# A whole-model kernel on one core: the ends and the beginnings of two attention blocks rearranged

## The reference

```python
for i in range(DEPTH):
    h  = half_ffn(h, ...);  hc = half_ffn(hc, ...)
    u  = modulated_norm(h, g[2], m, 3);  uc = modulated_norm(hc, g[2], mc, 3)
    if kind == 0: y, yc = diff_attention_mixer(u, uc, ...)     # p[:, 0] - lam * p[:, 1]
    elif kind == 1: y, yc = gqa_axial_mixer(u, uc, ...)        # q and k are rms-normed
    h = gated_residual(h, y, g[3], m, 3, 1.0)
    h = half_ffn(h, m, 6, ...)
    if ctx_out:                                                # layer 0 only
        hc = gated_residual(hc, yc, ...);  hc = half_ffn(hc, mc, 6, ...)

def attend(qb, kb, vb):                                        # DA, per head and query block
    sc = einsum('blhid,bkhid->bihlk', qb, kb) * scale
    p = softmax(sc);  p = p[:, 0] - lam_full * p[:, 1]
    o = einsum('bhlk,bkhd->blhd', p, vb)
    return rmsnorm(o, subln) * (1.0 - lambda_init)             # a norm per head
```

## Time and profile before

| | |
|---|---|
| median of three runs | 2476.23 us (2474.5 to 2476.89) |
| the profiled execution's own time | 2472.06 us |
| its span, first to last instruction | 2470.3 us |
| mean granted TensorE clock | 0.984 |
| busy: PE, DVE, ACT, POOL | 2349.1, 1479.4, 913.9, 1363.2 us |
| DMA, mean | 142 GB/s |
| DA, from the first rotary matmul to the last head's sum | 453.2 to 672.9 us |
| GA, from the first sum of squares to the last product with v | 1498.7 to 1597.3 us |

### The profile page before, as it was taken

How to read it: one execution, slowest core, us unless ns; L and a number is a source line. 1 busy time by engine, 2 the same in 40 slices (tenths; PEclk the granted TensorE clock), 3 DMA queues, 4 the chain that set the end, 5 groups by cost and what they waited for, 6 DMA issues and landing times.

```text
span 2470.3 us, 35964 instructions
## 1 busy us (share of the span) xinstructions
PE 2349.1 (95%) x14514; PEld 2073.8 (84%) x14514; DVE 1479.4 (60%) x2344; ACT 913.9 (37%) x1461; POOL 1363.2 (55%) x688
## 2 busy tenths in 40 slices
PE   6999999899899999999999997889989999999998
PEld 5887789677688777898778886789989999999998
DVE  6999896656569998968973045563235212563421
ACT  3222224444442222243222244444444444544443
POOL 4455465122144554554554451268868886466986
PEclk8999999999999999999999998999999999999999
DMA  6555452111125554525533321135536564344554
GB/s 270 196 187 185 145 194 83 60 60 52 37 84 196 193 182 152 185 98 186 180 111 90 101 83 61 68 132 185 178 113 205 179 193 146 101 147 144 190 181 135
DMA packets 97220, 350.09 MB, mean 142 GB/s; under 512 B 10912, under 2 KB 10912, under 8 KB 96800
## 3 DMA queue, kind: packets, MB, share of 16 engines
q1 hardware_dynamic: 97056, 347.81, 41.7%
HBM read 346.71 MB, written 1.05 MB: 141 GB/s over the span
## 4 chain that ended last, share of the span: by engine, by line
PE 50%; DVE 13%; issue 4%; ACT 2%; DMA 1%; POOL 1%; DVEq 0%; ACTq 0%
PE psum L1345 16%; PE psum L1349 15%; PE psum L1346 15%; DVE psum L962 8%; PE psum L1639 1%; DVE sq L1149 1%; POOL w_lo L650 1%; PE psum L1612 1%; DMA ada_lo<-in_ada_w 1%; ACT w_hi L670 0%; DVE gu_hi L1152 0%; DMA w_raw<-in_ffn_in 0%; PE psum L1620 0%; PE psum L1380 0%; DVE h L1058 0%
## 5 line engine op out<-in xcount | busy, mean ns | idle before, releaser
L650 POOL TENSOR_TENSOR w_lo<-w_raw,w_hi 128x1024 fp32r<-128x1024 f32 (+3 forms) x684 | 1363.0, 2011 | 1090.0 <-ACT w_hi L670 1089.2
L1345 PE MATMUL psum<-u_hi,w_hi 128*128 128x256 f32 (+1 forms) x2912 | 978.5, 336 | 20.1 <-DVE sq L1149 6.1
L1349 PE MATMUL psum<-u_lo,w_hi 128*128 128x256 f32 (+1 forms) x2912 | 950.9, 327 | 2.9 <-DVE u_lo L1044 2.9
L1346 PE MATMUL psum<-u_hi,w_lo 128*128 128x256 f32 (+1 forms) x2912 | 949.9, 326 | 0.0
L670 ACT ACTIVATE w_hi<-w_raw 128x1024 fp32r<-128x1024 f32 (+1 forms) x522 | 534.1, 1034 | 422.4 <-PE psum L1349 347.7
L1345 PEld LDWEIGHTS psum<-u_hi,w_hi 128*128 128x128 f32 x2912 | 558.5, 192 | 102.4 <-DVE sq L1149 26.6
L1349 PEld LDWEIGHTS psum<-u_lo,w_hi 128*128 128x128 f32 x2912 | 557.6, 191 | 49.9 <-DVE u_lo L1044 3.9
L1346 PEld LDWEIGHTS psum<-u_hi,w_lo 128*128 128x128 f32 x2912 | 558.7, 192 | 43.7 <-issue 2.9
L1345 PE MATMUL psum<-gu_hi,w_hi 128*128 128x256 f32 (+1 forms) x1188 | 379.3, 319 | 0.0
L1346 PE MATMUL psum<-gu_hi,w_lo 128*128 128x256 f32 (+1 forms) x1188 | 378.2, 318 | 0.0
L1349 PE MATMUL psum<-gu_lo,w_hi 128*128 128x256 f32 (+1 forms) x1188 | 378.1, 318 | 0.0
(11 more groups left out here) (144 smaller groups left out, 1965.9 us busy)
## 6 DMA issues: line engine op xcount, KB each, us to landing
w_raw<-in_ffn_in SPq DMA_DIRECT2D x264, 512.0 KB, 4.1
w_raw<-in_ffn_out SPq DMA_DIRECT2D x96, 448.0 KB, 3.4
ada_hi<-in_ada_w SPq DMA_DIRECT2D x48, 512.0 KB, 3.6
ada_lo<-in_ada_w SPq DMA_DIRECT2D x48, 512.0 KB, 3.5
w_raw<-in_ffn_out SPq DMA_DIRECT2D x48, 512.0 KB, 3.5
ada_out<-in_ada_w SPq DMA_DIRECT2D x32, 512.0 KB, 4.5
w_raw<-in_b_qkv SPq DMA_DIRECT2D x30, 512.0 KB, 3.5
w_raw<-in_da_in SPq DMA_DIRECT2D x24, 512.0 KB, 3.5
```

What stands on the lines that cost most here:

```text
L650: last = pool.tensor_tensor(w_lo[:, slot, w], w_raw[:, slot, w], w_hi[:, slot, w].bitcast(F32), ALU.subtract)
L1345: mm(out, w_hi[:, slot, w], x_hi, start=start and n == 0, stop=False)
L1346: mm(out, w_lo[:, slot, w], x_hi, start=False, stop=False)
L1349: last = mm(out, w_hi[:, slot, w], x_lo, start=False, stop=stop and n == len(ks) - 1)
```

## The change

Five edits, all around the two attention blocks of the first network; `b2` keeps its order.

1. **First phase.** DA gets a fifth tile, k of head 1, as an extra: its latent pass stands ahead of `h_sum`, its context pass behind those of the first four. GA runs k0, v0, k1, v1 (all of the keys and values) as its four and the latent q0 as its extra. The input tiles of GA lie in that order in memory. v1 is staged in an unused part of `q_st`.
2. **DA's last head.** Its units go latent, latent, context, context, and its end (`O`, `oss`) is done once for the latent half and once for the context half, the latter through bank 6.
3. **DA's output** begins with the latent pieces of tiles 2 and 3, ahead of the last k of tiles 0 and 1. The latent pieces of tiles 4 to 7 use banks 4 and 5 in turn, where they used 0, 1, 4, 5.
4. **Fillers.** DA's are spread over the last unit and behind, with none kept; GA begins a third output tile with the heads and keeps three.
5. **Heads.** ACT makes the heads of output tiles 4 and 5 of DA beside the last head's transposes, not in the output.

```diff
@@ -101,11 +101,14 @@
 def out_pieces(kind, tok):
 
     if tok == LAT:
-        return [(j, LAT, {"ffn": 4 + j % 2, "b2": j % 2, "ga": (0, 1, 4, 5)[j % 4]}[kind]) for j in range(CH)]
-    first, banks = (6, (4, 5, 0, 1)) if kind == "ffn" else (2, (4, 5, 0, 1))
-    tail = [(j, half) for half in halves(FULL) for j in range(first, CH)]
-    return [(j, FULL, 4 + j % 2 if kind == "ffn" else j) for j in range(first)] \
-        + [(j, half, banks[i % 4]) for i, (j, half) in enumerate(tail)]
+        banks = {"ffn": (4, 5), "b2": (0, 1), "ga": (0, 1, 2, 4, 5, 0, 1, 4)}[kind]
+        return [(j, LAT, banks[j % len(banks)]) for j in range(CH)]
+    if kind == "ffn":
+        tail = [(j, half) for half in halves(FULL) for j in range(6, CH)]
+        return [(j, FULL, 4 + j % 2) for j in range(6)] + [(j, half, (4, 5, 0, 1)[i]) for i, (j, half) in enumerate(tail)]
+    ctx = slice(0, CTX)
+    return [(2, LAT, 4), (3, LAT, 5), (0, FULL, 0), (1, FULL, 1)] \
+        + [(j, LAT, 4 + j % 2) for j in range(4, CH)] + [(j, ctx, (0, 1, 4, 5)[(j - 2) % 4]) for j in range(2, CH)]
...
-FILL_UNITS = 3
-FILL_KEPT = {"da": 4, "ga": 2, "b2": 0}
+FILL_UNITS = {"da": 1, "ga": 3, "b2": 3}
+FILL_KEPT = {"da": 0, "ga": 3, "b2": 0}
+EARLY = {"da": 2, "ga": 3, "b2": 2}
...
+            tiles = (2, 0, 3, 1) if h < DA_HEADS - 1 else (2, 3, 0, 1)
             sets.append({"s": h, "items": items, "q": items[:1], "k": items[1:2], "v": items[2:],
-                         "units": [{"qt": qt, "keys": keys, "ocol": qt * 128} for qt, keys in
-                                   ((2, TOK), (0, CTX), (3, TOK), (1, CTX))]})
+                         "units": [{"qt": qt, "keys": TOK if qt >= 2 else CTX, "ocol": qt * 128} for qt in tiles]})
     elif kind == "ga":
-        kv = None
+        kv = [[item("k", g, 0, FULL, norm=True, rope=True, par=g), item("v", g, 0, FULL, par=g)] for g in range(GA_KV)]
         for h in range(GA_HEADS):
             g = h // (GA_HEADS // GA_KV)
-            items = []
-            if h % (GA_HEADS // GA_KV) == 0:
-                kv = [item("k", h, 0, FULL, norm=True, rope=True, par=g % 2), item("v", h, 0, FULL, par=g % 2)]
-                items += kv
+            items = [it for pair in kv for it in pair] if h == 0 else []
             items.append(item("q", h, 0, LAT, norm=True, rope=True, par=0, place=h % 3))
-            sets.append({"s": h, "items": items, "q": items[-1:], "k": kv[:1], "v": kv[1:],
+            sets.append({"s": h, "items": items, "q": items[-1:], "k": kv[g][:1], "v": kv[g][1:],
                          "units": [{"qt": qt, "keys": TOK, "ocol": qt * 128} for qt in (2, 3)]})
...
+        if kind == "da" and st["s"] == DA_HEADS - 1:
+            st["outs"] = [{"s": st["s"], "tok": LAT, "after": U - 3}, {"s": st["s"], "tok": slice(0, CTX), "after": U - 1}]
+        else:
+            st["outs"] = [{"s": st["s"], "tok": FULL if kind == "da" else LAT, "after": U - 1}]
+    for n, x in enumerate(x for st in sets for x in st["outs"]):
+        x["n"] = n
+    for n, it in enumerate(it for st in sets for it in st["items"] if it["norm"]):
+        it["sq"] = n
...
+    items = [it for st in sets for it in st["items"]]
+    first, extra = items[:4], items[4:4 if kind == "b2" else 5]
+    begun = set((it["idx"], k) for it in first + extra for k in range(0, CH, 2))
+    add("first", (first, extra))
...
+    lead += parts(ahead)[:{"da": 2, "ga": 4, "b2": 0}[kind]]
     for part in lead:
-        begun.add(part[0]["idx"])
+        begun.add((part[0]["idx"], part[1]))
         add_part(part)
         prepare_due()
...
+        filler += [(d, k, min(k + 2, last), last) for d in range(2, EARLY[kind]) for k in range(0, last, 2)]
     kept = FILL_KEPT[kind]
...
+        if it["what"] == "v" and it["g"] == 0 and it["s"] == 1 and it["idx"] == 3:
+            return q_st[:, 1, 0:n]
...
+        if kind == "da" and s == DA_HEADS - 1 and tok != LAT:
+            return SUMS
...
-                    for it in x:
+                    for it in x[0] + x[1]:
                         evacuate(it)
...
+                    if kind == "da" and u["set"]["s"] == DA_HEADS - 1:
+                        heads_to(min(b["t_out"] + 4 + u["U"] - u["set"]["first_unit"], b["t_out"] + RING - 1))
...
-                    return len(tiles) - n if n == full[-1] else 1
+                    return len(tiles) - n + sum(tok == LAT for _, _, tok in extra) if n == full[-1] else 1
...
-            for t, bank, _ in extra:
-                run(1, t, bank, range(CH)).then_inc(tile_used, 1)
+            for t, bank, tok in extra:
+                if tok != LAT:
+                    run(1, t, bank, range(CH)).then_inc(tile_used, 1)
...
+                if b["kind"] == "da":
+                    ctx_ready = lambda k: pe.wait_ge(MS["da"]["olo_ready"], k + 2)
...
-                early = b["kind"] in ("da", "ga") and i < 2
+                early = b["kind"] in ("da", "ga") and j < EARLY[b["kind"]]
...
-    X["ga_in"] = ga[[n for g in range(GA_KV) for n in (GA_HEADS + g, GA_HEADS + GA_KV + g, *range(per * g, per * g + per))]]
+    X["ga_in"] = ga[[n for g in range(GA_KV) for n in (GA_HEADS + g, GA_HEADS + GA_KV + g)] + list(range(GA_HEADS))]
```

97 lines of the change are left out of this document (50 added, 47 removed).

## The result

The changed kernel takes 2481.71 us (median of 7 executions, 2480.38 to 2485.11), the one before 2475.02 in the same series (2472.99 to 2479.2): ratio 1.0026, interval 1.0016 to 1.0035, so 6.4 us slower (4.0 to 8.7). 2478.5 was forecast, 2.2 us slower than before, with "within 0.2%" (5 us) as the likeliest case. Gains and losses are worked out from these ratios throughout (0.0001 is 0.25 us); the plain difference of the two medians is 6.7. The profiled execution took 2481.71 (span 2479.9). That of before took 2472.06, and all 31 executions of before timed in the next series took longer than that (2472.11 to 2479.73, median 2476.43). The two traces are 9.65 us apart, where the ratio gives 6.4: some 3 us between the traces are luck of the execution.

What follows compares the result with a forecast made beforehand. PE, 95% busy, bounds the blocks' middles; chains through DVE and ACT bound starts and ends. -0.6 + 0.5 + 1.3 + 0.7 + 0.3 = +2.2 us on median 2476.23, about 2478.5; 8-in-10 range 2468.5 to 2488.

Steps and rivals of the forecast that it cites:

- likeliest case: Whole kernel: time within 0.2% (5 us) of before, the sum of the terms with its errors; chance 0.47.
- DA's start: Start of DA: latent pass of the fifth tile fits the idle time; 0.6 us gained, bounds 2.8 gained and 1.5 lost.
- DA's last head: Units 28 to 31 of DA, with no filler between their scores: 0.5 us lost, bounds 3 gained and 2 lost.
- DA's output: Output of DA: 1.3 us of new wait at latent piece 6, bounds 0.4 and 2.5.
- GA's start: Start of GA: unit 2 delayed 13.6 us against 12.9 saved in the middle; 0.7 lost, bounds 5.3 gained, 3 lost.
- k0's Ln: Sign in GA's start: ACT comes to k0's Ln some 7 us later than before.
- GA's end: End of GA: 0.7 us gained by fillers and third output tile, 1.0 lost; net 0.3 lost, bounds 0.8 and -2.
- Rival 1: DA and GA: filled gaps count in full, 11 us gained, 2465; middle version 2471; chance 0.22.
- Rival 2: GA's start: ACT's queue decides; GA loses 5 to 7 us, DA 2 to 3, 2484; chance 0.31.
- Rival 3: GA's first phase: k1 and v1 could put off DVE's work on the context half; no size, called nearly excluded.
- the 2 us at unit 29's scores: Sign in DA's last head: about 2 us of PE idle time between scores of units 28, 29 and 30.
- the 1 to 2 ahead of piece 6: Sign in DA's output: 1 to 2 us of PE idle time before latent piece 6.

Runs made afterwards that it cites:

- e1: Changed kernel with the DA edits alone, GA as before the change; ratio to before 1.0007, 1.7 us slower.
- e10: e4 with the sums of squares of k0, q0 and k1 also put ahead of the transposes of v0 and v1; ratio to before 1.0007.
- e3: Changed kernel with v7's transposes right behind unit 28's scores instead of unit 30's; ratio to before 1.0016, changed kernel 1.0026.
- e8: Changed kernel without ACT's heads of DA's output tiles 4 and 5 beside the last head's transposes, made in the output instead; ratio to before 1.0027.
- e9: Changed kernel with added unused matmuls where PE stands idle in DA's last head; ratio to before 1.0023.
- e4: Changed kernel with ACT's three heads of GA's first phase moved behind the Ln and Exp of k0, q0 and k1; ratio to before 1.0009.
- e7: Changed kernel without GA's third early output tile, two fillers kept; ratio to before 1.0023.
- e12: e10 with v7's transposes right behind unit 28's scores and the heads of DA's output tiles 6 and 7 one piece later; ratio to before 0.9983.
- e2: Changed kernel with the GA edits alone, DA as before the change; ratio to before 1.0016, 4.0 us slower.
- e11: e10 with DA's last head and output as before the change, DA's fifth tile kept; ratio to before 0.9987, 3.2 us faster.

## Why the prediction was right, and where it was not

The direction was right and the time lies in the range, 3.2 us above the likeliest one. The size was not: 6.4 us slower (4.0 to 8.7) where 2.2 were forecast, so the likeliest case, within 5 us, is met only by the lower end of the interval. In the traces DA is 6.8 us longer and GA 5.5; together that is nearly twice the 6.4 of the ratio, so part of what follows is what these two executions happened to get. The terms, by the profiled executions:

- **DA's start**, forecast 0.6 gained. Shown: nothing that can be told from zero (0.3 by the means above; from `h_sum` to unit 28's scores, unit 1 included, 210.2 us as a mean of the twelve, 208.4 to 211.0, against 210.3 and 210.7). That context passes run no sooner was right. Part of the scatter is the clock behind the sum: 0.68 granted in the changed kernel (438.5 to 443), 1.00 in e1 and e10.
- **DA's last head**, forecast 0.5 lost, bounds 3 gained and 2 lost. Measured 4.8 (6.2 less the 1.39 at piece 6), beyond the bound; 1.7 for all of DA by the ratio of e1. This is the step that failed. Unit 29 came 5.26 us behind unit 28 (forecast 5.29) and unit 30 10.35 (10.2), but unit 31 22.0 where 16.1 was forecast (18.9 before the change). The text took unit 31's scores to follow from head 6's end alone. It left out that v7's copy, which the old order did ahead of these steps, now stands behind two of them on DVE while PE waits for it in order: 4.01 us (e3, e8). And it charged half clock with 0.8 us, where it took some 3: the last head had 17 us of it, and was 3.2 us shorter without (e9).
- **DA's output**, forecast 1.3 lost at piece 6, measured 1.39 there, by the chain as told (loads, heads, square, add). The bound of 2.5 was too small: 3.54 in e1, with the add stretched to the end of POOL's second tile, not its first.
- **GA's start**, forecast 0.7 lost: a delay of 13.6 against 12.9 saved. The delay was 14.75, the steps close: k0's Ln forecast 22.3 behind the sum and found 21.45, first transposes 12.0 later and found 11.7, from these to unit 2's scores 3.2 and found 4.61. The half clock came elsewhere than forecast: none in the context phase, where 1.7 us had been charged, but 13.8 us of it up to unit 2 (8.3 before), from 1515.35 on, among the idle times of the chain. That ACT's queue opens the chain is shown (e4). The 12.9 was the worse number. From unit 2 to unit 6 it was 30.16 - 18.22 = 11.9, and from unit 6 to 15, where nothing was changed, 2.1 us came back. In before PE had waited 4.2 us of 41.4 there, now 5.5 of 43.5: a pair of units takes 9.3 us through DVE's probabilities,

```profile
1561.46 0.66 PE L1647 MATMUL psum<-tab,pcomb 128*128 128x128 f32 x4 [0.69 <-DVE pcomb L1229]
...
1570.81 0.66 PE L1647 MATMUL psum<-tab,pcomb 128*128 128x128 f32 x4 [0.70 <-DVE pcomb L1229]
...
1580.15 0.66 PE L1647 MATMUL psum<-tab,pcomb 128*128 128x128 f32 x4 [0.69 <-DVE pcomb L1229]
```

and before, the stretch of k1 and v1 had let DVE get ahead (it had 56 steps left in this stretch, now 59), so that its first units behind it ran faster. That reading of the 2.1 us is argued from the rows; no run tests it. The earlier trace rows show 30.00 busy of 30 for 1519 to 1549 alone; the text read "the middle" from them. So GA's start lost about 5, not 0.7. The idle 7.02 us that was filled did not shorten the way to the sum, as forecast.
- **GA's end**, forecast 0.3 lost, measured 0.57, and 0.55 by e7.
- **Rival 1** (gaps count in full) is excluded: the gaps were filled and nothing came of it. **Rival 2** named the right queue. Its condition (k0's Ln later than 1511, a delay of over 17) was not met, yet its direction was right for GA, for another reason: the saved matmuls were worth 9.9, not 12.9. **Rival 3** is out: from the sum over the latent half to that over the context half it is 21.29 us before and 21.23 after in GA.

Of the signs named, k0's Ln (6.6 us later for 7), the 2 us at unit 29's scores (only 1.0 at unit 30's) and the 1 to 2 ahead of piece 6 (1.39) were as told. The idle time ahead of GA's `h_sum` was none for 1 to 2, and that between the context phase and unit 2 grew from 7.6 to 13.4 us, not to 15. One of the sums is wrong: the bounds for a gain add to 11.5 (2.8 + 3 - 0.4 + 5.3 + 0.8), not 12.9; those for a loss do add to 11.

The errors all lay on one side. That the range (2468.5 to 2488) held them owes something to its width and to the kernel losing by the ratio only half of what the two blocks of the traces show.

## What to carry to other kernels

When a step is moved on one engine, list for each engine what now stands ahead of the steps that were *not* moved; v7's copy was not in the change at all. Before a stretch is called bound by PE, read the window in which the work is saved and the one behind it, to where the chain of units is back at its own pace. And a head or a load put behind a copy in an in-order queue should go behind the first step of the latency chain: that alone gave back 4.2 of the 6.4 us by the ratios. e12 keeps every edit of the change, with the four repairs, and is 4.2 us faster than before.

## What the runs showed of the chip

- Idle times of up to 5.0 us between short bursts in DA's last head came with half clock in every order tried but the one with added matmuls: 0.83 to 0.93 granted for 52 to 61 us, 0.97 in the best, 1.00 with the added matmuls (idle times of 0.44, 1.49 and 1.65 were left). In the changed kernel the clock fell with no idle time longer than 2.00 us ahead of it. PE's busy time there goes with it, 43.68 us at 0.97 and 49.28 at 0.83 for two matmul rows more. The same order of work (before, e2, e11) got 0.97, 0.93 and 0.88 in three executions, so a difference of up to 4 us between two traces of this stretch is not evidence.
- DVE steps on SBUF alone took up to 2.86 us beside POOL's tile, those with two tensors 0.41 to 0.75 without it, a small one on 128x2 up to 1.98 for 0.17. Steps with a PSUM input kept their time, for instance 0.41 for a rotary step and 0.75 for `o_raw`.
